# Output projection by token tiles with all its weights on chip, and the norms of the last three token halves behind the last value product

## The chip, the cores and the metric

The kernel runs on one core of a Trainium2 chip. The metric is device time in microseconds for one execution of the whole program; lower is better. The core has five engines that run side by side, each through its own list of instructions in order: TensorE (PE; its weight loads are shown apart as PEld), VectorE (DVE), ScalarE (ACT), GpSimd (POOL) and SyncE (SP), which here only issues DMAs. They are held together by semaphores that the kernel writes out by hand.

## What is computed

One decoder layer over 1024 tokens and 16 meta tokens of width 1024: a norm, one input projection, eight heads of stick-breaking attention (64 wide) and four heads of a gated linear recurrence (128 wide), a norm over each head, one output projection that is added to the input, a second norm, and a SwiGLU feed-forward of width 2816.

```python
o_sb = stick_breaking_attention(sb_q, sb_k, sb_v)            # 8 heads x 64
o_sb = group_rmsnorm(merge_heads(o_sb), sb_norm_g, SB_HEADS)
o_hg = hgrn2_chunkwise(hg_q, hg_k, hg_i, log_f)              # 4 heads x 128
o_hg = group_rmsnorm(merge_heads(o_hg), hg_norm_g, HG_HEADS) * jax.nn.silu(hg_g)
mix = jnp.concatenate([o_sb, o_hg], axis=-1) @ w_out
h = h + mix
u2 = rmsnorm(h, norm2_g)
ffn = (jax.nn.silu(u2 @ w_gate) * (u2 @ w_up)) @ w_down
return rmsnorm(h + ffn, final_norm_g)                        # the 1024 tokens
```

All matmuls are of float32 precision: each operand is split into a rounded high part and the rest as a low part (type fp32r), and a product is three matmuls, high with high, high with low, low with high.

## The kernel before

**The last pair of heads.** Attention runs over pairs of heads and, in a pair, over 14 pieces of a query block (`PIECES`, n = 0 to 55). TensorE makes scores (L973), transposes the weights of a piece (`turn`, L990) and multiplies them with the values (`values`, L1010); ScalarE makes two sigmoids of the scores (L1104, L1107) and copies the transposes out (L1131, L1133); VectorE scans a running product (L1158) and weighs (L1165). A half of the tokens of a pair, number e = 0 to 7, is complete every seven pieces. Its head norm then goes: ScalarE squares the output and copies it to `mixed` (`out_evac`, L1114, L1115), TensorE sums (L1040), ScalarE takes the root (`head_norm_scalar`, L1054), VectorE inverts and widens (`head_norm_widen`, L1061, L1063), TensorE transposes (L1047), VectorE scales `mixed` (`head_norm_finish`, L1071). `SUMS_AT` and `SPREAD_AT` (L130, L131) say at which piece; e = 5 and 6 fall into the last pair, e = 7 behind the loop. Finished halves of `mixed` are split into `tok_hi` (ScalarE, L1085) and `tok_lo` (VectorE, L1090), two at a piece (`SPLIT_AT`, L1078): 15 of 16 in the loop, the last behind it.

**The output projection.** Behind the loop TensorE runs 32 groups of 12 matmuls (`out_group` at L1928, `out_part`, L335 to L337) as four passes c = 0 to 3 over all eight token tiles t: the passes 0 and 1 make the left 512 columns (first the recurrence heads' half of the contraction, then the attention heads'), 2 and 3 the right 512. A pass uses one chunk of `w_out` of 1 MB, called ("O", c). It is loaded by SyncE into `w_raw` (L477), copied to `w_hi` by ScalarE (`high_chunk`, L482), and its rest goes to `w_lo` by VectorE (`low_chunk`, L500). There are two slots, so chunk 2 is split when pass 0 is over and chunk 3 when pass 1 is. The next load into `w_raw` waits for the split before. After pass 1 and pass 3 VectorE adds a token tile's bank to `h_res` (`add`, L1649), which GpSimd has filled with x after the last value product (L1309).

**The second norm.** For a token tile whose row is complete: ScalarE squares with a running sum and takes the root (`stats`, L1437, L1440), VectorE inverts and scales (`scale`, L1654, L1658), TensorE transposes (`second_transposes`, L1947), ScalarE copies out twice, rounded and whole (`high`, L1449, L1452), VectorE makes the low part (`low`, L1671). All rows are complete only in pass 3. SyncE spills `h_res` to memory (L1209), since its place is used again.

**The feed-forward's first half.** A scheme of seven products for four (`P1` to `P7`, `PRODUCTS` at L135) is applied to blocks of the gate and up weights, n = 0, 2, ... gate and n = 1, 3, ... up. A product is 12 matmuls (L1977, L1979, L1980). Each needs a block of weights, or a sum of blocks (`weight_sums`, `weight_sum4`: L1715, L1718, L1721, L1727), rounded by ScalarE (`block_high`, L1393) and completed by VectorE (`block_low`, L1705) into a ring of ten, and tokens or sums of tokens (t1 to t4). The token sums are made by VectorE over all tiles at once (`token_sum`, L1696), rounded by ScalarE (`high_t`, L1463); the low parts are made by VectorE for t2 (L1685) and by GpSimd for t3 and t4 (L1320). Raw blocks come through two buffers, and the load for n = 2 waits for `block_low(12)`, the last use of n = 0. P1(2) also waits for `weigh_f(0, 2)` (L1762), the product of the gated part with the bank that it writes anew. The order of all this is written out by hand, once for each engine; that of TensorE is

```python
for c in range(4):
    for t in range(TT):
        ...
        out_group(c, t)
        ...
        if c == 3 and t >= 4:
            second_transposes(t - 3)
...
second_transposes(5); p1(0); second_transposes(6); p2(0); second_transposes(7)
p1(1); p2(1); p5(0); p5(1); p3(0); p3(1); p6(0); p6(1); p7(0); p7(1); p4(0)
```

(the last two lines stand one call to a line in the code). After them the loop over n = 2 to 21 takes its steady form.

## Time and profile before

| | |
|---|---|
| median of 3 runs | 1391.59 us (1389.67 to 1391.77) |
| profiled execution | 1388.97 us, its span 1387.2 us |
| TensorE busy | 1317.5 us, 95% |
| VectorE, ScalarE, GpSimd busy | 59%, 40%, 3% |
| mean granted clock of TensorE | 0.99 |

The profile is of one execution. Times in its rows count from the start of the span; durations are of one instruction, or of a merged row from its first start to its last end. Two instructions of one engine overlap a little, so a row's duration is larger than the distance from start to start. "[7.15 <-DVE h_res L1762]" says that the engine sat idle for 7.15 us before, and what it seems to have waited for.

### The profile page before, as it was taken

What the parts mean: (1) busy time and instruction counts of PE and PEld (TensorE: products, weight loads), DVE (VectorE), ACT (ScalarE), POOL (GpSimd) and SP (SyncE); (2) the same over time, 40 slices, a digit from 0 to 9 for tenths busy, and PEclk for the clock granted to TensorE, in tenths of its full rate; (3) what the DMA queues carried; (4) which work ended last, traced back from release to release, by engine and by line L of the source; (5) the groups of instructions that cost most, each with busy time, mean ns of one, the idle gap of its engine ahead of it and who ended that gap; (6) DMA issues with size and microseconds to landing.
All of it is one profiled execution on the core that took longest, in us unless ns stands there. A gap on an engine that the chain in (4) does not pass through costs nothing.

```text
span 1387.2 us, 23036 instructions
## 1 busy us (share of the span) xinstructions
PE 1317.5 (95%) x9428; PEld 1086.9 (78%) x9428; DVE 819.3 (59%) x1334; ACT 554.8 (40%) x1027; POOL 38.7 (3%) x64
## 2 busy tenths in 40 slices
PE   5999999999899999879987999999999999999998
PEld 5898989898567767458866888888888888888886
DVE  6376766763787565852486665655666646335413
ACT  6323332331676455851374333333333334324311
POOL 4000000000000000010003000000000000000000
PEclk9999999999999999999998999999999999999999
DMA  6211111011001000031322222122222239626601
GB/s 199 61 32 31 32 31 32 32 32 31 2 32 32 2 32 2 32 138 62 110 86 76 92 84 82 63 92 91 91 91 71 74 121 343 212 75 217 231 23 61
DMA packets 77496, 112.18 MB, mean 81 GB/s; under 512 B 3776, under 2 KB 52928, under 8 KB 77392
## 3 DMA queue, kind: packets, MB, share of 16 engines
q1 hardware_dynamic: 74528, 100.74, 21.8%
q0 software_dynamic: 2864, 9.97, 2.0%
q8 instruction: 75, 1.23, 0.4%
q14 instruction: 29, 0.24, 0.1%
HBM read 90.78 MB, written 19.92 MB: 80 GB/s over the span
## 4 chain that ended last, share of the span: by engine, by line
PE 88%; ACT 6%; DVE 4%; issue 2%; DMA 1%; ACTq 0%; DVEq 0%; POOLq 0%
PE ps L1977 10%; PE ps L1980 9%; PE ps L1979 9%; PE ps L323 8%; PE ps L325 8%; PE ps L324 8%; PE ps L2065 6%; PE ps L2066 6%; PE ps L2064 6%; PE ps L1010 3%; PE ps L973 2%; PE ps L614 2%; PE ps L990 2%; PE ps L335 2%; PE ps L337 2%
## 5 line engine op out<-in xcount | busy, mean ns | idle before, releaser
L323 PE MATMUL ps<-a_hi,w_hi 128*128 128x352 f32 (+2 forms) x576 | 207.8, 361 | 7.5 <-DVE a_lo L441 2.9
L325 PE MATMUL ps<-a_hi,w_lo 128*128 128x352 f32 (+2 forms) x576 | 200.0, 347 | 0.0
L324 PE MATMUL ps<-a_lo,w_hi 128*128 128x352 f32 (+2 forms) x576 | 199.9, 347 | 0.0
L323 PEld LDWEIGHTS ps<-a_hi,w_hi 128*128 128x128 f32 x576 | 109.2, 190 | 20.2 <-DVE a_lo L441 3.3
L1977 PE MATMUL ps<-a_hi,w_hi 128*128 128x512 f32 x288 | 114.4, 397 | 9.9 <-DVE h_res L1762 7.2
L325 PEld LDWEIGHTS ps<-a_hi,w_lo 128*128 128x128 f32 x576 | 109.1, 189 | 8.3
L324 PEld LDWEIGHTS ps<-a_lo,w_hi 128*128 128x128 f32 x576 | 109.3, 190 | 7.3
L1979 PE MATMUL ps<-a_lo,w_hi 128*128 128x512 f32 x288 | 113.5, 394 | 0.0
L1980 PE MATMUL ps<-a_hi,w_lo 128*128 128x512 f32 x288 | 113.4, 394 | 0.0
L2064 PE MATMUL ps<-a_hi,w_hi 128*128 128x512 f32 x288 | 112.0, 389 | 0.0
L2065 PE MATMUL ps<-a_lo,w_hi 128*128 128x512 f32 x288 | 112.0, 389 | 0.0
L2066 PE MATMUL ps<-a_hi,w_lo 128*128 128x512 f32 x288 | 112.0, 389 | 0.0
L1158 DVE TENSOR_TENSOR_SCAN beta<-beta,ones 128x272 f32<-128x272 f32 (+5 forms) x112 | 92.9, 870 | 15.7 <-ACT beta L1104 15.7
L500 DVE TENSOR_TENSOR w_lo<-w_raw,w_hi 128x2048 fp32r<-128x2048 f32 (+1 forms) x22 | 41.8, 1902 | 75.3 <-ACT w_hi L482 75.3
L1977 PE MATMUL ps<-t_hi,w_hi 128*128 128x512 f32 x208 | 81.0, 390 | 0.6 <-POOL t_lo L1320 0.6
L1980 PE MATMUL ps<-t_hi,w_lo 128*128 128x512 f32 x208 | 80.9, 389 | 0.0
L1979 PE MATMUL ps<-t_lo,w_hi 128*128 128x512 f32 x208 | 80.9, 389 | 0.0
L1977 PEld LDWEIGHTS ps<-a_hi,w_hi 128*128 128x128 f32 x288 | 55.0, 191 | 22.5 <-DVE h_res L1762 7.6
L1980 PEld LDWEIGHTS ps<-a_hi,w_lo 128*128 128x128 f32 x288 | 54.9, 191 | 11.7
L1979 PEld LDWEIGHTS ps<-a_lo,w_hi 128*128 128x128 f32 x288 | 55.1, 191 | 11.4
L2064 PEld LDWEIGHTS ps<-a_hi,w_hi 128*128 128x128 f32 x288 | 54.1, 188 | 11.3
L2065 PEld LDWEIGHTS ps<-a_lo,w_hi 128*128 128x128 f32 x288 | 54.1, 188 | 11.2
(274 smaller groups left out, 2557.3 us busy)
## 6 DMA issues: line engine op xcount, KB each, us to landing
w_raw<-in_w_in_dram SPq DMA_DIRECT2D x24, 512.0 KB
w_raw<-in_w_gate_dram SPq DMA_DIRECT2D x11, 1024.0 KB, 5.5
h_res<-in_w_up_dram SPq DMA_DIRECT2D x11, 1024.0 KB, 5.4
f_spill<-h_res SPq DMA_DIRECT2D x44, 256.0 KB, 2.0
h_res<-in_w_down_dram SPq DMA_DIRECT2D x22, 512.0 KB, 5.7
w_raw<-f_spill SPq DMA_DIRECT2D x30, 256.0 KB, 4.2
w_raw<-in_w_down_dram SPq DMA_DIRECT2D x11, 512.0 KB, 4.9
h_norm<-in_w_down_dram SPq DMA_DIRECT2D x11, 512.0 KB, 5.7
```

Of the source, the lines that this page charges most:

```text
L323: nc.tensor.matmul(psum, wh, ah, start=k == 0, stop=False)
L324: nc.tensor.matmul(psum, wh, al, start=False, stop=False)
L325: last = nc.tensor.matmul(psum, wl, ah, start=False, stop=k == KT - 1)
L500: last = nc.vector.tensor_tensor(w_lo[:, s, c], w_raw[:, c], w_hi[:, s, c].bitcast(F32), ALU.subtract)
L1010: last = nc.tensor.matmul(dst, v, probs_t[:, par, i * P:(i + 1) * P], start=hi == width and i == 0, stop=lo == 0 and i == len(tiles) - 1)
L1158: nc.vector.tensor_tensor_scan(c, c, ones[:, 0:1].to_broadcast([P, hi - lo]), begin, ALU.mult, ALU.mult).then_inc(scanned.sem, 1)
L1977: nc.tensor.matmul(psum, wh[:, c], yh[:, k], start=start and k == 0, stop=False, skip_group_check=not start)
L1979: nc.tensor.matmul(psum, wh[:, c], yl[:, k], start=False, stop=False, skip_group_check=not start)
L1980: last = nc.tensor.matmul(psum, wl[:, c], yh[:, k], start=False, stop=k == UNIT - 1, skip_group_check=not start)
L2064: nc.tensor.matmul(psum, fh[:, a], tok_hi[:, q % 8, half], start=start, stop=False)
L2065: nc.tensor.matmul(psum, fh[:, a], tok_lo[:, q % 8, half], start=False, stop=False)
L2066: return nc.tensor.matmul(psum, fl[:, a], tok_hi[:, q % 8, half], start=False, stop=stop)
```

## The change

Three things are changed together.

*The last norms.* For e = 5, 6 and 7 ScalarE no longer takes the root in its place; for 5 and 6 it copies the eight sums to `kept`. Behind the last value product it takes the roots of all three, VectorE inverts and widens all three, TensorE transposes twelve times after the third projection group, and VectorE finishes the three halves, which are then split (three splits behind the loop instead of one).

*The output projection.* Chunks 2 and 3 of `w_out` get slots of their own (in the places of t3 and t2), and the groups run in the order `OUT_SEQ`: the left columns of tiles 0 to 3 as two passes, tile 4's left, then the right columns tile by tile for 0 to 4, then tiles 5, 6 and 7 each with all four groups. Banks follow `ADD_BANK`. The sums, the norm and the transposes of a tile run as soon as its row is complete; `n2_rows` has two rows instead of four.

*The first products.* The ring of ten is turned by eight places, `sum1` has a second place for n = 1, the token sums are made tile by tile, and the low parts of t3 and t4 are made by VectorE. The written orders of ScalarE and VectorE between the projection and the steady loop are new.

```diff
-SPREAD_AT = {n + 2: e for n, e in SUMS_AT.items()}
+SPREAD_AT = {n + 2: e for n, e in SUMS_AT.items() if e < 5}
+LAST_HALVES = [6, 5, 7]
...
+OUT_SEQ = [(t, c) for c in (0, 1) for t in range(4)] + [(4, 0), (4, 1)] + \
+    [(t, c) for t in range(4) for c in (2, 3)] + [(4, 2), (4, 3)] + [(t, c) for t in (5, 6, 7) for c in range(4)]
...
+ADD_BANK = dict(zip(ADDS, [0, 1, 2, 3, 4, 5, 6, 7, 5, 6, 7, 4, 5, 6, 7, 4]))
...
+        def last_norms_scalar(act):
+            act.wait_ge(s_sum.sem, s_sum.done(8))
+            nc.scalar.activation(kept_of(7), bank(7, 8), ACT.Sqrt, scale=1.0 / SB_DIM, bias=eps).then_inc(s_root.sem, 1)
+            nc.scalar.activation(kept[:, 0:16], kept[:, 0:16], ACT.Sqrt, scale=1.0 / SB_DIM, bias=eps)\
+                .then_inc(s_root.sem, 1)
+
+        def last_norms_widen(dve):
+            dve.wait_ge(s_root.sem, s_root.done(9))
+            nc.vector.reciprocal(kept, kept).then_inc(s_inv.sem, 1)
+            dve.wait_ge(s_inv.sem, s_inv.done(6))
+            for e in LAST_HALVES:
+                nc.vector.tensor_copy(WIDE[e].rearrange("p (c t) -> p c t", c=2 * UNIT),
...
         def head_norm_scalar(act, e, psum):
             act.wait_ge(s_sum.sem, s_sum.done(e + 1))
+            if e >= 5:
+                nc.scalar.activation(kept_of(e), psum, ACT.Copy).then_inc(s_root.sem, 1)
+                return
...
-                low_t(Y12, t3_hi, t3_lo, UNIT, t3_done)
-                low_t(Y22, t4_hi, t4_lo, 2 * UNIT, t4_done)
...
-                high_chunk(act, ("O", 1))
-                high_chunk(act, ("O", 2), (o_proj, TT))
-                high_chunk(act, ("O", 3), (o_proj, 2 * TT))
+                high_chunk(act, ("O", 2), (t_done, 2 * NP))
+                act.wait_ge(m_lo.sem, 16)
+                high_chunk(act, ("O", 3), (t_done, 2 * NP))
...
+                for t in range(3):
+                    high_t(Y12, t3_hi, t3_sum, t3_high, t)
+                hold_p1(1)
+                block_high(12)
+                high_t(Y11, t2_hi, t2_sum, t2_high, 3)
+                high_t(Y12, t3_hi, t3_sum, t3_high, 3)
                 act.wait_ge(t2_done.sem, t2_done.done(UNIT))
-                high_t(Y22, t4_hi)
-                hold_u2(1)
+                act.wait_ge(t4_sum.sem, t4_sum.done(UNIT))
+                for t in range(4):
+                    high_t(Y22, t4_hi, t4_sum, t4_high, t)
+                hold_p5(0)
+                hold_p5(1)
                 block_high(13)
...
+                block_low(6)
+                add(7, 1)
                 scale(7)
...
+                low(7)
+                low_t1(3)
+                token_sums(3)
                 block_low(10)
                 block_low(11)
+                for t in range(3):
+                    low_t(Y12, t3_hi, t3_lo, t3_high, t3_done, t)
                 block_low(12)
+                low_t(Y11, t2_hi, t2_lo, t2_high, t2_done, 3)
+                low_t(Y12, t3_hi, t3_lo, t3_high, t3_done, 3)
+                c11(1)
+                for t in range(4):
+                    low_t(Y22, t4_hi, t4_lo, t4_high, t4_done, t)
                 c22(0)
                 c12(0)
                 block_low(13)
...
+                for n, (t, c) in enumerate(OUT_SEQ):
+                    if n == 1:
+                        head_norm_tensor(pe, 7, "sums", bank(7, 8))
+                    if n == 3:
+                        last_norms_tensor(pe)
+                    if n == 2 * UNIT:
+                        pe.wait_ge(s_mixed.sem, 8)
+                    out_group(t, c)
+                    if c == 3 and 1 <= t <= 4:
+                        second_transposes(t - 1)
+                    if c == 1 and t >= 5:
+                        second_transposes(t - 1)
...
-                second_transposes(5)
                 p1(0)
-                second_transposes(6)
                 p2(0)
                 second_transposes(7)
```

## Rows read from the trace of the kernel before

**Rows 1.** The page: busy us, share of the span, instructions.

```profile
PE 1317.5 (95%) x9428; PEld 1086.9 (78%) x9428; DVE 819.3 (59%) x1334; ACT 554.8 (40%) x1027; POOL 38.7 (3%) x64
```

**Rows 2.** Windows: busy us (instructions) by engine, clock, DMA share and GB/s.

```profile
560.00:607.00 47.00, 32.54 (x571) 20.64 (x569) 38.68 (x63) 40.58 (x88) 0.00 (x0) 0.93 0.07 24
607.00:705.00 98.00, 94.20 (x468) 77.70 (x468) 37.12 (x50) 28.60 (x49) 4.98 (x9) 1.00 0.36 129
705.00:770.00 65.00, 54.93 (x228) 43.99 (x229) 51.67 (x69) 35.39 (x65) 14.28 (x9) 0.89 0.19 66
770.00:1100.00 330.00, 330.00 (x1457) 273.27 (x1456) 201.07 (x313) 115.86 (x208) 0.00 (x0) 1.00 0.26 84
```

**Rows 3.** TensorE's waits, 540 to 830: us in total, times, longest.

```profile
PE ps L1977 <- DVE h_res L1762: 7.2, 1, 7.2
PE ps L1947 <- ACT y_first L1452: 2.4, 1, 2.4
...
PE ps L1977 <- DVE a_lo L1678: 1.4, 1, 1.4
...
PE ps L1977 <- POOL t_lo L1320: 0.6, 1, 0.6
```

**Rows 4.** Timeline of ScalarE in the last pair: start, us, line, operation, tiles.

```profile
564.10 1.28 ACT L1054 ACT_TABLE_LOAD   x1
565.39 0.27 ACT L1054 ACTIVATE small<-ps,small 128x8 f32<-128x8 f32 x1
...
566.17 1.28 ACT L1104 ACT_TABLE_LOAD   x1
...
594.79 1.19 ACT L1085 ACTIVATE a_hi<-mixed 128x512 fp32r<-128x512 f32 x2
```

**Rows 5.** Timeline of VectorE there: a stretch without a wait between first and last.

```profile
567.99 1.81 DVE L1158 TENSOR_TENSOR_SCAN beta<-beta,ones 128x384 f32<-128x384 f32 x2 [1.63 <-ACT beta L1104]
...
571.83 0.74 DVE L1071 SCALAR_TENSOR_TENSOR mixed<-mixed,small,ps 128x512 f32<-128x512 f32 x1
...
592.57 0.43 DVE L1063 COPY gain<-small 128x512 f32<-128x512 f32 x1
...
602.22 0.68 DVE L1090 TENSOR_TENSOR a_lo<-mixed,a_hi 128x512 fp32r<-128x512 f32 x1
```

**Rows 6.** Timeline of TensorE at the projection's start, and its four transposes.

```profile
607.89 0.47 PE L335 MATMUL ps<-w_hi,a_hi 128*128 128x512 f32 x1 [1.33 <-issue]
...
616.77 0.60 PE L1047 MATMUL ps<-ident,gain 128*128 128x128 f32 x4
617.13 0.48 PE L335 MATMUL ps<-w_hi,a_hi 128*128 128x512 f32 x1
```

**Rows 7.** DMA issues: destination, source, count, KB each, median us to landing.

```profile
w_raw<-in_w_gate_dram SPq DMA_DIRECT2D x11, 1024.0 KB, 5.5
...
h_res<-in_x_dram POOLq DMA_DIRECT2D x8, 512.0 KB, 8.0
```

**Rows 8.** Timeline of VectorE between projection and steady loop.

```profile
620.66 2.29 DVE L500 TENSOR_TENSOR w_lo<-w_raw,w_hi 128x2048 fp32r<-128x2048 f32 x1 [1.11 <-ACT w_hi L482]
...
681.48 1.29 DVE L1658 SCALAR_TENSOR_TENSOR n_rows<-h_res,small,gain 128x1024 f32<-128x1024 f32 x1
...
734.54 1.78 DVE L1705 TENSOR_TENSOR w_lo<-w_raw,w_hi 128x512 fp32r<-128x512 f32 x1
...
750.90 2.68 DVE L1762 TENSOR_TENSOR h_res<-h_res,h_norm 128x512 f32<-128x512 f32 x4
```

**Rows 9.** Timeline of ScalarE in the same stretch.

```profile
678.02 1.06 ACT L1437 ACTIVATE n_junk<-h_res 128x1024 f32<-128x1024 f32 x1 [2.24 <-DVE h_res L1649]
...
745.10 0.63 ACT L1393 ACTIVATE w_hi<-w_raw 128x512 fp32r<-128x512 f32 x1 [5.81 <-DMA w_raw<-in_w_gate_dram]
```

**Rows 10.** Windows, columns as in rows 2: after a short and after a long wait.

```profile
592.00:594.00 2.00, 0.63 (x4) 0.42 (x4) 1.97 (x5) 1.99 (x6) 0.00 (x0) 1.00 0.00 0
...
752.00:760.00 8.00, 5.17 (x12) 4.08 (x13) 6.47 (x11) 0.74 (x2) 0.00 (x0) 0.51 0.38 139
```

More of the change, by code:

```diff
@@ L182, in hybrid_layer @@
         table_load = small[:, 72:73]
+        kept = small[:, 72:96]
         meta_decay = sb("meta_decay", [P, 2 * META])
@@ L310, in hybrid_layer @@
         UNITS = [(h, half) for h in range(HG_HEADS) for half in range(2)]
-        slots = [(w_hi[:, 0], w_lo[:, 0]), (w_hi[:, 1], w_lo[:, 1])]
-        OUT_BANKS = [0, 1, 2, 3, 4, 6, 5, 7]
+        slots = [(w_hi[:, 0], w_lo[:, 0]), (w_hi[:, 1], w_lo[:, 1])] + \
+            [[t[:].rearrange("p k n -> p (k n)") for t in pair] for pair in ((t3_hi, t3_lo), (t2_hi, t2_lo))]
         def turned_group(weights, tile, cols, psum, a_hi=act_hi, a_lo=act_lo, steps=range(KT)):
@@ L1177, in attention_vector @@
                     nc.vector.tensor_copy(turned_to(1, w), turned(1, w)).then_inc(pt_second.sem, 1)
-                if n - 1 in SUMS_AT:
+                if SUMS_AT.get(n - 1, 5) < 5:
                     head_norm_widen(dve, SUMS_AT[n - 1])
@@ L1231, in _ @@
                 load_raw(0)
-                for t in range(4):
+                for t in range(2):
                     spill_h(t)
@@ L1237, in _ @@
                 load_raw(1)
-                for t in range(4, TT):
+                for t in range(2, TT):
                     spill_h(t)
@@ L1469, in _ @@
+                stats(0)
+                stats(1)
+                high(0)
+                stats(2)
+                high(1)
+                stats(3)
+                high(2)
+                stats(4)
+                high(3)
+                act.wait_ge(n2_normed.sem, n2_normed.done(4))
+                act.wait_ge(x_came[2].sem, 32)
+                act.wait_ge(x_came[3].sem, 32)
                 block_high(0)
                 block_high(1)
-                stats(0)
-                stats(1)
@@ L1762, in weigh_f @@
                     nc.vector.tensor_tensor(u, u, src, ALU.mult).then_inc(weighed[i].sem, 1)
-                low_chunk(dve, ("O", 1))
+                add(0, 0)
                 low_chunk(dve, ("O", 2))
-                for t in range(TT):
-                    add(0, t)
+                add(1, 0)
+                add(2, 0)
+                add(3, 0)
                 low_chunk(dve, ("O", 3))
+                add(4, 0)
                 dve.wait_ge(gain2.sem, 16)
+                add(0, 1)
+                scale(0)
@@ L1770, in _ @@
+                add(1, 1)
+                scale(1)
+                low(0)
+                add(2, 1)
+                scale(2)
+                low(1)
+                add(3, 1)
+                scale(3)
+                low(2)
+                add(4, 1)
+                scale(4)
+                low(3)
                 block_low(0)
                 block_low(1)
-                add(1, 0)
                 weight_sums(0)
                 weight_sum4(0)
-                add(1, 1)
-                scale(0)
@@ L1777, in _ @@
-                add(1, 2)
-                scale(1)
-                low(0)
-                add(1, 3)
-                scale(2)
-                add(1, 4)
-                scale(3)
-                low(1)
-                add(1, 5)
-                scale(4)
-                low(2)
-                add(1, 6)
-                scale(5)
-                low(3)
+                add(5, 0)
+                low(4)
+                first_sums(1)
+                low_t1(0)
+                token_sums(0)
@@ L1791, in _ @@
+                add(5, 1)
+                scale(5)
+                add(6, 0)
+                low(5)
+                low_t1(1)
+                token_sums(1)
+                add(6, 1)
+                scale(6)
                 block_low(2)
-                add(1, 7)
-                scale(6)
-                low(4)
                 block_low(3)
-                scale(7)
-                low(5)
-                block_low(4)
-                weight_sums(1)
-                low(6)
-                low_t1(0)
@@ L1802, in _ @@
-                weight_sum4(1)
-                block_low(5)
-                low(7)
-                low_t1(1)
-                low_t1(2)
-                low_t1(3)
-                token_sum(0)
-                block_low(6)
+                block_low(4)
+                add(7, 0)
+                second_sum(1)
+                weight_sum4(1)
+                low(6)
+                block_low(5)
+                low_t1(2)
+                token_sums(2)
+                block_low(6)
+                add(7, 1)
```

253 lines of the change are left out of this document (124 added, 129 removed).

## Prediction

> **What bounds the kernel now.** I read the page's busy shares first, then the granted clock and busy time by stage, then TensorE's waits, then the timelines of the places where it waits. TensorE is busy 95% of the span [rows 1], so a change can only pay where it is idle or slow. By stage [rows 2] that is two places: the last pair of heads (560 to 607 us: TensorE 32.5 us of 47, ScalarE 40.6, VectorE 38.7) and the first products of the feed-forward (705 to 770: 54.9 of 65, clock 0.89). The output projection between them is full (94.2 of 98), and from 770 on TensorE is busy without a gap (330.0 of 330). So the projection itself, 384 matmuls, has nothing to give: the change keeps its matmuls and their shapes. What it can give lies on either side of it.
>
> On the right side TensorE waits 7.2 us for one VectorE product, 2.4 us for ScalarE, 1.4 us for VectorE's `a_lo` and 0.6 us for GpSimd's `t_lo` [rows 3], with 0.9 us of issue between; after the long wait twelve matmuls start every 0.43 us instead of 0.23.
>
> **Part 1: the norms of the last three token halves.** In the last pair two head norms (e = 5 and 6) fall into the loop. Each makes ScalarE load the Sqrt table, take a 128x8 root and load the Sigmoid table back: 1.28 + 0.27 + 1.28 us [rows 4]. The change puts a 128x8 Copy in the root's place; no trace shows it, the nearest row is the 128x8 root itself, 0.27 us, so the root and the copy cancel and four loads go, 5.1 us. (Bounds: a Copy that cost nothing adds 0.5, one that cost as much as a 128x512 split, 0.6 us, takes 0.7.) One of ScalarE's splits (0.52 us from start to start, half of the x2 row in [rows 4]) also leaves the loop. A second one left stood behind the last sigmoids and was hidden. ScalarE loses 5.6 us.
>
> Does the stage's end move by that? The chain of waits goes through ScalarE from 564 to 599.6 almost without a break, but VectorE is busy without a break from 567.99 to 602.9 as well [rows 5]. Its first scan waited for ScalarE's sigmoid behind the two table loads, and so starts 2.5 us earlier. Within the stretch it loses two finishes (0.74 us each, 0.66 from start to start), one widening (reciprocal and copy, 0.56) and one split (0.60): 2.5 us. VectorE therefore gives 5.0 us and ScalarE 5.6, and the turning of the last pieces lags behind the scans by 2 to 5 us, which absorbs the difference. I take 5.4 us, bounds 3.5 (VectorE sets it and a piece's turn is lost) and 6.2. Two finishes, two widenings and eight transposes come back after the last value product. They are covered: TensorE has three projection groups of 2.73 us to run from 607.89 before it needs them [rows 6], in which today ScalarE and VectorE only wait; three widenings of 0.43 and a larger reciprocal end some 6 us after that start, and the transposes come at 8.6 to 8.9. The transposes themselves are on TensorE: four cost 0.44 us here (616.77 to 617.13, and a slower first matmul), so eight more cost 0.8. What stands behind them is tight: the fourteenth split ends 12.7 us after the start and group (0,1), now fifth, wants it at 12.5 to 13.0, a wait of 0 to 0.3 us that I leave at nothing; each further us of delay in the chain transposes, finish, split would be paid in full.
>
> The Trainium skill ("ScalarE: Activation LUTs", What ACT_TABLE_LOAD costs) agrees with the 1.28 us of a load but adds a drain of about 1.38 us to each switch; here the root starts 1.29 us after the load and the load follows the copy before it at once, so no drain shows. By the page's 2.66 us four switches would be worth 10.6 us (estimate) instead of 5.1. I go by the rows.
>
> **Part 2: weights on chip.** Chunks 2 and 3 get buffers of their own, so their splits no longer wait for the projection's passes. They must now arrive early, since token tile 0 wants all four. Counting from the first projection matmul: chunk 1 is split on ScalarE by 5.7 and on VectorE by 8.1 (1.9 us, and 2.3 in [rows 8]); the load of chunk 2 is issued then, but eight loads of x of 512 KB, 8.0 us each to land, fill the DMA engines until about 12 us [rows 7], so I give it 7.5 us instead of the 5.5 of a load of 1 MB. Chunk 2 is on chip at 19.9, chunk 3 (5.5 + 1.9 + 2.3) at 29.7. TensorE needs chunk 2 at 29.1 and chunk 3 at 31.9. Cost nothing, with 2.2 us of cover; a load later by more than that is paid in full.
>
> **Part 3: sums, norms and the first products.** The adds, statistics (1.06 us Square and a root, 1.48 to the end [rows 9]) and scalings (1.29 [rows 8], 1.45 with the reciprocal) of tokens 0 to 4 now run under groups of later tiles, where before all eight stood in the last pass. GpSimd's eight `t_lo` go to VectorE, at 0.60 us from start to start: 4.8 us more for VectorE. But while GpSimd ran them, three `block_low` took 1.78 us each instead of 0.68 [rows 8]; that goes, 3.3 us.
>
> I walked the written order of the engines from the first projection matmul, each step at the durations above. The same walk for the old order gives P1(2) its start at 754.2 against 754.8 in the trace. In the new order TensorE has these stalls left:
> - before transposes 5, 0.6 us (add, statistics and scaling of tile 5 against two groups);
> - before P1(0), 1.6: the last group's sum has a `block_low` before it on VectorE, and P1 waits for all sixteen sums;
> - before P3(0), 1.9: ScalarE's copy of P5(0) is queued behind four t4 roundings, which wait for VectorE's last t2 part;
> - before P1(2), 3.2. After P7(0) VectorE has thirteen operations in line (two sums with banks, three `block_low`, three weight sums, four products, then the product P1(2) waits for), 8.4 us at 0.60 to 0.72 and 0.3 for the hand-overs, against 5.5 us of P7(1) and P4(0).
>
> This last stall is 7.2 us today because the gate block for it is asked for after `block_low(12)` ends at 739.7, lands 5.4 us later [rows 9], and only then come the rounding, the Sigmoid table and the four products (2.68 us for four products in [rows 8]). In the new order `block_low(12)` ends 113 us after the first projection matmul, where it now ends at 132, so the block has landed before P3 is over and the table is loaded under P3(1).
>
> The clock: after the 7.2 us wait it stood at half (1.2 GHz) for nearly all of 752 to 760 [rows 10], P1(2) took 5.2 us instead of 2.73. After the 2.1 us wait at 591 to 593 it stayed at 2.4 GHz [rows 10]. A wait of 3.2 us lies between: 0 to 2.5 us, I take 1.2.
>
> **The sum.** Today's losses: waits 2.4 + 0.9 + 1.4 + 0.6 + 7.2 = 12.5, low clock 1.5 (seven matmuls of P1(0)) + 2.5, together 16.5. New: 0.6 + 1.6 + 1.9 + 3.2 + 1.2 = 8.5, and 0.8 of transposes. Right side: 16.5 - 9.3 = 7.2 us. With part 1: 7.2 + 5.4 = 12.6. The walk without rounding the small gaps gives 8.2 for the right side; I take 13 in all. Behind P1(2) nothing changes: the steady loop is TensorE's. The profiled execution took 1389.0 us (span 1387.2 and 1.8 around it) and would take 1376.0; the median of the runs is 1391.6, 2.6 above it, and would become 1378.6.
>
> **The rivals.**
> - *The stage of the last heads does not give what the table loads cost.* VectorE's unbroken stretch speaks for it, ScalarE's part in the chain against. If only the 2.5 us ahead of the first scan come through: 13 - 2.9 = 10.1, 1381.5.
> - *The stall before P1(2) stays*, since its last link is VectorE's order behind P7(0), with the clock at half again and 5 us or more idle: 2 to 4 us less, 1381 to 1383. For it: VectorE's queue ahead of it is longer than before by the t4 parts. Against: those end 13 us before P7(0) does.
> - *The stalls close almost wholly* and the clock stays up: 4 us more, 1374.5. The walk's steps are accurate to some 0.6 us each, and three stalls are below 2.
> - *Slower: the weights come late.* From 29.1 us on, tile 0 stands first and the whole order is behind it. If chunk 2's load were held back by the loads of x and chunk 3's by the same amount, beyond 2.2 us of cover for both together, the wait is paid once, before group (0,3). To end over 0.2% slower the two loads would have to be later by 13 + 2.2 + 2.8 = 18 us, 9 us each and so 14.5 to 16.5 us long instead of the 5.5 to 8.0 that [rows 7] show. With 6 us more it is 1382, with 18 us 1394.5.
> - *It does nothing*: TensorE's work is the same, and if the reordering only moved the waits, 1391.
>
> **How the numbers follow.** Forecast 0.66; closing stalls 0.10; the heads giving half 0.09; the stall staying 0.09; late weights, mild 0.02; nothing 0.02; late weights, slower 0.02. The range takes in the closing stalls, both unknown costs and the two cases around 1382: 1373 to 1384. A time within 0.2% (2.8 us, about what a measurement of this kernel can tell from no change) needs two of the bad cases at once or a load late by some 12 us: 0.03. Slower 0.03, faster 0.94.
>
> **What would show it.** Right: in 560 to 607 only one Sqrt load remains (the last), VectorE's stretch starts near 565.5, and the first projection matmul comes at 602.5. No TensorE wait for `w_lo` in the projection, transposes between the groups. No GpSimd `t_lo`, every `block_low` at 0.68. The gate block for n = 2 is issued about 18 us earlier against the projection's start, and the wait before P1(2) is about 3 us. Wrong: a wait of TensorE before group (0,3) for chunk 3, a granted clock below 1 inside the projection, or a stage of heads that ends later than 604.

## The result, and the profile of the changed kernel

The changed kernel takes 1380.1 us (median of four, 1379.3 to 1381.5) against 1390.9 (1389.7 to 1391.8) beside it: ratio 0.9924, 95% interval 0.9907 to 0.9941, 10.8 us faster. The forecast was 1378.6, 13 us faster. Measured again on another chip it was 1379.6 against 1390.0, ratio 0.9919 (0.9896 to 0.9941). The profiled execution took 1381.45 us, the longest of its four, with a span of 1379.7 us and a mean granted clock of 0.985; that of the kernel before took 1388.97 us, near the short end of its times (1388.4 to 1393.8 over all rounds). So the two profiles lie only 7.5 us apart.

Busy us, share and instructions of each engine, to set beside [rows 1]:

```profile
PE 1319.8 (96%) x9428; PEld 1089.1 (79%) x9428; DVE 821.6 (60%) x1349; ACT 549.9 (40%) x1024; POOL 24.8 (2%) x56
```

TensorE's work is the same, GpSimd has lost 14 us of it, ScalarE 5, VectorE has 2 more. TensorE's waits in the changed kernel, from 520 to 800 us (us in total, times, longest), against [rows 3]:

```profile
PE ps L2044 <- issue: 3.7, 2, 2.0
PE ps L2044 <- DVE h_res L1811: 3.0, 1, 3.0
...
PE ps L2015 <- DVE n_rows L1703: 0.5, 1, 0.5
```

The wait of 7.2 us before P1(2) is 3.0 us. The one for `y_first`, the one for `a_lo` and the one for GpSimd's `t_lo` are gone. The two waits of `issue`, before P1(0) and P3(0), have grown from 0.9 and 0.4 to 1.7 and 2.0 us, and there is one of 0.5 us before the transposes of tile 5. The timeline has these, and the projection's start (start us, us, line, operation, tiles, idle before):

```profile
604.53 0.77 PE L343 MATMUL ps<-w_hi,a_hi 128*128 128x512 f32 x1 [1.33 <-issue]
```

```profile
704.15 0.47 PE L2044 MATMUL ps<-a_hi,ring_more 128*128 128x512 f32 x1 [1.68 <-issue]
...
723.60 0.47 PE L2044 MATMUL ps<-a_hi,w_hi 128*128 128x512 f32 x1 [1.98 <-issue]
```

The first of these rows, the projection's first matmul, already holds the surprise. It took 0.47 us in [rows 6] and takes 0.77 here. The granted clock of three stretches says why; it is the column before the DMA share:

```profile
600.00:608.00 8.00, 5.90 (x39) 4.58 (x36) 0.56 (x1) 2.86 (x4) 3.39 (x7) 0.58 0.24 82
724.00:728.00 4.00, 4.00 (x12) 3.11 (x11) 0.41 (x1) 2.11 (x3) 0.00 (x0) 0.57 0.24 79
748.00:752.00 4.00, 4.00 (x13) 3.09 (x12) 3.15 (x6) 0.00 (x0) 0.00 (x0) 0.57 0.12 45
```

Behind the waits around the last values (1.9, 0.8 and 1.3 us), behind P3(0)'s 1.98 us and behind P1(2)'s 3.0 us TensorE ran at half its clock (1.2 GHz) for most of 7, 4 and 4 us. In the one profile of the kernel before, the clock was at 1.00 at the start of the projection.

To say where the time went I cut each profile at three places: the last copy of `bq` at 560.53 in the kernel before (the start of the last pair), the first projection matmul, and ScalarE's copy of the bank behind P1(2), which is the row at 760.21 before and at 752.16 after. In the changed kernel these two ScalarE rows are:

```profile
562.48 0.60 ACT L582 ACTIVATE bq<-ps 128x512 f32<-128x512 f32 x1 [2.08 <-PE ps L333]
...
752.16 0.60 ACT L1442 ACTIVATE h_norm<-ps 128x512 f32<-128x512 f32 x1 [5.45 <-PE ps L2047]
```

| kernel | up to last pair | last pair | projection to P1(2) | rest |
|---|---|---|---|---|
| before | 560.5 | 47.4 | 152.3 | 627.0 |
| changed | 562.5 | 42.1 | 147.6 | 627.5 |
| changed, again | 561.0 | 43.1 | 147.5 | 627.6 |
| norms alone | 560.3 | 42.1 | 154.2 | 627.0 |
| tiles alone | 561.1 | 49.0 | 145.3 | 627.0 |
| low parts on GpSimd | 560.0 | 42.3 | 150.7 | 627.0 |
| chunk 3 late | 560.8 | 43.1 | 153.3 | 627.6 |
| new order | 559.9 | 42.3 | 143.9 | 627.5 |
| fillers everywhere | 560.9 | 41.5 | 143.4 | 627.6 |
| fillers around heads | 560.4 | 41.5 | 144.8 | 627.6 |
| fillers before gate | 560.0 | 42.2 | 145.6 | 627.6 |
| order and fillers | 560.3 | 41.5 | 141.8 | 627.6 |
| order and fillers, again | 559.9 | 41.5 | 141.2 | 627.6 |

The first column moves by 2.6 us although nothing in front of it is edited in any of these kernels: it is longer where a low stretch of the clock falls into the loop over heads (near 352 and 492 us in the first profile of the changed kernel). So the stages are to be compared, not the spans: 5.3 us came from the last pair and 4.7 from projection to P1(2), against 5.4 and 7.2 to 8.2 forecast.

### The profile page after: what moved, and what is told of

It is laid out like the page before. It is cut to its first block, busy times and chain, and to the rows that moved or that the text cites. A ratio compares the mean times of both kernels' runs of the same rounds, so it can differ in the third digit from the quotient of the medians.

```text
span 1379.7 us, 23039 instructions
## 1 busy us (share of the span) xinstructions
PE 1319.8 (96%) x9428; PEld 1089.1 (79%) x9428; DVE 821.6 (60%) x1349; ACT 549.9 (40%) x1024; POOL 24.8 (2%) x56
## 4 chain that ended last, share of the span: by engine, by line
PE 91%; ACT 3%; DVE 3%; issue 2%; DMA 1%; ACTq 0%; DVEq 0%; POOLq 0%
PE ps L2044 10%; PE ps L2047 10%; PE ps L2046 10%; PE ps L331 9%; PE ps L333 8%; PE ps L332 8%; PE ps L2130 6%; PE ps L2131 6%; PE ps L2129 6%; PE ps L1020 3%; PE ps L983 2%; PE ps L343 2%; PE ps L624 2%; PE ps L344 2%; PE ps L345 2%
## 5 line engine op out<-in xcount | busy, mean ns | idle before, releaser
L2044 PE MATMUL ps<-a_hi,w_hi 128*128 128x512 f32 x280 | 110.6, 395 | 5.0 <-DVE h_res L1811 3.0
L332 PEld LDWEIGHTS ps<-a_lo,w_hi 128*128 128x128 f32 x576 | 109.6, 190 | 7.2
L2129 PE MATMUL ps<-a_hi,w_hi 128*128 128x512 f32 x288 | 112.0, 389 | 0.0
L2130 PE MATMUL ps<-a_lo,w_hi 128*128 128x512 f32 x288 | 112.0, 389 | 0.0
L2131 PE MATMUL ps<-a_hi,w_lo 128*128 128x512 f32 x288 | 112.0, 389 | 0.0
L2047 PE MATMUL ps<-a_hi,w_lo 128*128 128x512 f32 x280 | 110.3, 394 | 0.0
L2046 PE MATMUL ps<-a_lo,w_hi 128*128 128x512 f32 x280 | 110.0, 393 | 0.0
L510 DVE TENSOR_TENSOR w_lo<-w_raw,w_hi 128x2048 fp32r<-128x2048 f32 (+1 forms) x20 | 37.3, 1864 | 63.4 <-ACT w_hi L492 63.3
L1227 DVE COPY probs_t<-ps 128x384 f32<-128x384 f32 (+2 forms) x44 | 25.3, 575 | 63.5 <-PE ps L1000 63.2
L2129 PEld LDWEIGHTS ps<-a_hi,w_hi 128*128 128x128 f32 x288 | 54.0, 188 | 11.3
L2130 PEld LDWEIGHTS ps<-a_lo,w_hi 128*128 128x128 f32 x288 | 54.1, 188 | 11.2
```

The lines of the kernel that those rows point to most:

```text
L332: nc.tensor.matmul(psum, wh, al, start=False, stop=False)
L510: last = nc.vector.tensor_tensor(lo_[:, c], w_raw[:, c], hi_[:, c].bitcast(F32), ALU.subtract)
L2044: nc.tensor.matmul(psum, wh[:, c], yh[:, k], start=start and k == 0, stop=False, skip_group_check=not start)
L2046: nc.tensor.matmul(psum, wh[:, c], yl[:, k], start=False, stop=False, skip_group_check=not start)
L2047: last = nc.tensor.matmul(psum, wl[:, c], yh[:, k], start=False, stop=k == UNIT - 1, skip_group_check=not start)
L2129: nc.tensor.matmul(psum, fh[:, a], tok_hi[:, q % 8, half], start=start, stop=False)
```

## The experiments

**The two parts apart.** The first kernel has the norms finished late and everything else as before:

```diff
-SPREAD_AT = {n + 2: e for n, e in SUMS_AT.items()}
+SPREAD_AT = {n + 2: e for n, e in SUMS_AT.items() if e < 5}
...
```

> The kernel before with the part on the norms alone: the last three token halves of heads are finished together behind the last value product, in their own banks; the projection by groups of two halves, chunks 2 and 3 of w_out split as before, and GpSimd's token parts stay. My theory: the stage of the last pair gets 5.3 us shorter, as it did in the whole change, eight more transposes behind it cost 0.8 us, so 1390.9 becomes about 1386.4 (1385.5 to 1388; at the upper end if the low clock at the start of the projection comes with this part, 1.7 us). One Sqrt load between the last pair's softmax and the first projection matmul instead of five. Rival 1 (the stage gains only because the projection's evacuations by tiles make room there): 0 to -1.5 us. Rival 2 (this part is the whole gain, the tiles give nothing): -10 us or more, 1381.

Measured: 1386.9 us against 1391.1, ratio 0.9967 (0.9955 to 0.998), 4.6 us by the ratio (2.8 to 6.3). The last pair is 5.3 us shorter, as in the whole change. From the projection to P1(2) it is 1.9 us longer, and that arises ahead of P1(0), which starts 2.3 us later against the projection's start: the transposes (0.8 forecast) and a low clock at the start. Its first projection matmul:

```profile
602.32 0.77 PE L337 MATMUL ps<-w_hi,a_hi 128*128 128x512 f32 x1 [1.33 <-issue]
```

That is 0.77 again. VectorE's wait before P1(2) is untouched (7.2 us).

The second kernel has the norms of before in the changed kernel:

```diff
-SPREAD_AT = {n + 2: e for n, e in SUMS_AT.items() if e < 5}
+SPREAD_AT = {n + 2: e for n, e in SUMS_AT.items()}
...
-                        last_norms_tensor(pe)
+                        head_norm_tensor(pe, 7, "spread", bank(7))
...
```

> The changed kernel with the norms of before: every token half's norm is finished inside the loop over heads, the last one alone behind it; the projection by token tiles, its early chunks and VectorE's token parts stay as changed. My theory: the two parts are independent, so the gains of this run and of the norms alone add up to the whole (10.8 us within 1 us); from first projection matmul to the last product group the walk is 4.7 us shorter, as in the whole change, or 6 if the low clock at the start of the projection belongs to the norms. 1385 to 1386.5. Rival 1 (the parts need one another: the late norms delay the first group by tiles, so that its gain is eaten): -2 us or less, 1389. Rival 2 (the tiles are the whole gain): -9 us or more, 1382.

Measured: 1383.9 us, ratio 0.9952 (0.9936 to 0.9969), 6.7 us. Its own stage is 7.0 us shorter than before (152.3 to 145.3) and 2.3 us shorter than in the whole change: its profile has no low clock behind P3(0), which is worth 1.6 us (the table further down), and P1(0) starts 0.7 us sooner, with eight transposes fewer ahead of it. Its last pair is 1.7 us longer than before, with more low clock inside (0.84 from 560 to 600 us, before 0.91). Its first projection matmul, and the window around it:

```profile
610.09 0.77 PE L343 MATMUL ps<-w_hi,a_hi 128*128 128x512 f32 x1 [1.33 <-issue]
```

```profile
607.00:614.00 7.00, 5.43 (x21) 4.30 (x22) 0.10 (x1) 2.40 (x4) 3.82 (x8) 0.52 0.30 116
```

So the low clock at the start of the projection also comes with the norms of before. That the change brought it is not shown: it stands in all nine profiles of kernels that have the change or a part of it and no added matmuls ahead of the projection, and the only profile of the kernel before, which lacks it, is of one execution. The two parts add up: 4.6 + 6.7 = 11.3, the whole change 10.8 and 11.3. Within the width of these intervals neither part needs the other, and neither is the whole gain. The part that I had costed at 5.4 - 0.8 is worth 4.6.

**GpSimd's low parts.** The eight operations go back to GpSimd:

```diff
...
-                for t in range(4):
-                    low_t(Y22, t4_hi, t4_lo, t4_high, t4_done, t)
+                for t in range(4):
+                    pool_low(Y22, t4_hi, t4_lo, t4_high, t4_done, t)
...
```

> The changed kernel with the low parts of the token tiles (eight operations, t3 and t4) on GpSimd again as before, everything else as changed. Theory A (VectorE's subtractions and GpSimd's disturb one another: block_low took 1.78 us beside GpSimd's work and 0.68 without): the block_low operations beside them take 1.78 us again, and c22(0) and the low parts of t4 come 2 to 3 us later than now; the waits before P3(0) and P1(2) grow, 1 to 4 us slower than the changed kernel, 1381 to 1384. Rival B (that contention was covered: in that stretch VectorE stands idle for 14.7 us and gets rid of eight operations of 0.60 us): within 0.5 us, or up to 2 us faster, because the queue before P1(2) loses four operations.

Measured: 1382.6 us against 1379.6 for the changed kernel on the same chip, 3.0 us slower (ratios to before 0.9944, 0.9926 to 0.9961, and 0.9919, 0.9896 to 0.9941; the intervals overlap a little, the single times, 1381.7 and more against 1381.1 and less, do not). GpSimd, VectorE and TensorE of this kernel (the three timelines):

```profile
713.99 6.72 POOL L1369 TENSOR_TENSOR t_lo<-h_res,t_hi 128x512 fp32r<-128x512 f32 x4 [7.39 <-ACT t_hi L1513]
```

```profile
716.09 1.78 DVE L1759 TENSOR_TENSOR ring_more<-w_raw,ring_more 128x512 fp32r<-128x512 f32 x1
...
717.79 1.77 DVE L1759 TENSOR_TENSOR ring_more<-h_res,ring_more 128x512 fp32r<-128x512 f32 x1
...
719.49 1.77 DVE L1759 TENSOR_TENSOR w_lo<-w_raw,w_hi 128x512 fp32r<-128x512 f32 x1
```

```profile
724.66 0.76 PE L2049 MATMUL ps<-a_hi,w_hi 128*128 128x512 f32 x1 [4.35 <-issue]
```

While GpSimd runs, each `block_low` takes 1.78 us, as in [rows 8]; without it 0.69. The wait before P3(0) is 4.35 instead of 1.97 us, 2.4 more, and nothing later gives that back. The path is VectorE's last t2 part (721.17, against P1(0) 2.4 us later than in the changed kernel), ScalarE's four t4 roundings, which wait for it, and the copy of P5(0) behind them. Theory A holds, with its place: the contention is on the path through P3(0), not before P1(2), whose wait stays 3.0 us. The Trainium skill ("SBUF — State Buffer", SBUF: two separate sides) says that a VectorE operation with two SBUF inputs and a GpSimd operation that reads SBUF exclude one another for a whole instruction. The trace agrees: VectorE's operations take 1.1 us more than their 0.7, and GpSimd's four take 6.7 us, where its next four, with VectorE idle, take 5.0.

**Weights that are late.** ScalarE's rounding of chunk 3 waits until eleven projection groups are done, the last of them (0,2), just ahead of the first that wants the chunk (the expectation calls it the third group, which it is of tile 0 alone):

```diff
-                high_chunk(act, ("O", 3), (t_done, 2 * NP))
+                high_chunk(act, ("O", 3), (o_proj, 11))
```

> The changed kernel with one wait changed: ScalarE's rounding of chunk 3 of w_out waits for the third group of the projection instead of the last softmax sums, so its low part comes about 4.3 us later than the first product that wants it (the cover in the changed kernel is 2 to 3 us). Nothing is added or left out. Theory A (weights that are late are paid for in full, since TensorE bounds this stage): a wait for w_lo of 4 to 5 us before that group, with a low clock behind it 1.7 more, 4 to 6.5 us slower than the changed kernel, 1384 to 1386.5. Rival B (the lag is taken up by the waits before P1(0), P3(0) and P1(2), 6.7 us in all, which are there in any case): less than 2 us slower.

Measured: 1385.7 us, 6.1 us slower than the changed kernel on the same chip (ratio to before 0.9968). TensorE's timeline, and the window behind the wait:

```profile
642.05 0.79 PE L343 MATMUL ps<-t_hi,a_hi 128*128 128x512 f32 x1 [4.68 <-DVE t_lo L510]
```

```profile
636.00:648.00 12.00, 7.32 (x22) 5.46 (x21) 3.24 (x3) 1.91 (x1) 0.00 (x0) 0.72 0.29 89
```

The stage from projection to P1(2) is 5.9 us longer than in the changed kernel (153.3 and 147.5). By the start times it is 4.7 of wait and 2.8 for the low stretch behind it, less 1.6 because this profile has no low clock behind P3(0). The three later waits stay at 1.7, 2.0 and 3.0 us, so they took up nothing. A late weight is paid in full, as the prediction's slower rival had it; only the weights were not late in the changed kernel.

**The low clock.** Added matmuls keep TensorE running where it waits. They write a bank that is free there and compute nothing of the result:

```diff
+        def keep_busy(count, psum, source):
+            for _ in range(count):
+                nc.tensor.matmul(psum, source[:, 0:P], source[:, 0:HALF], start=True, stop=True)
```

> The changed kernel with added matmuls of 128x512 that write a bank nobody reads afterwards, placed where TensorE waits: 8, 3 and 5 around the last pair of heads, 6 before P1(0), 8 before P3(0), 12 before P1(2). They compute nothing of the result. Theory A (the low clock after each wait is what my sum left out, 5 us in three stretches: 601 to 608, 724 to 728, 748 to 752): the granted clock stays at 1.00 behind the three waits and the kernel gets 3.4 to 5 us faster than the changed one, 1375 to 1377. Rival B (the low stretches cost nothing, because VectorE or ScalarE bounds the work just behind each wait too): within 0.7 us of the changed kernel, 1380. Rival C (the fillers stand in the way of the products that they precede: 0.216 us each at most at the full clock beyond the wait): 1 to 2 us slower, 1382.

Measured: 1375.0 us, ratio 0.9889 (0.9872 to 0.9906), against 0.9924 and 0.9919 for the changed kernel: 4.2 to 4.9 us faster than it. The clock at the three places (windows of this kernel; 716 to 724 and 736 to 748 hold P3(0) and P1(2)):

```profile
596.00:608.00 12.00, 12.00 (x106) 8.85 (x107) 3.70 (x9) 5.58 (x8) 4.22 (x8) 1.00 0.33 124
716.00:724.00 8.00, 7.85 (x35) 6.23 (x34) 5.17 (x9) 4.66 (x8) 0.00 (x0) 1.00 0.42 131
736.00:748.00 12.00, 11.72 (x52) 9.38 (x51) 10.14 (x17) 5.17 (x10) 0.00 (x0) 1.00 0.41 133
```

The clock stays at full speed, and the stage takes 143.4 us instead of 147.6. The waits themselves are not shorter, only filled. So the low clock cost 4.2 us of this stage, and 0.6 more in the last pair (42.1 to 41.5). Theory A, and rivals B and C fall.

What each stretch costs can be read from the starts of the same matmuls in several profiles (us; "low" where a low stretch falls in):

| kernel | projection to P1(0) | to P3(0) | to P1(2) | to ScalarE's copy |
|---|---|---|---|---|
| changed | 99.62 low | 19.45 | 23.91 low | 4.65 low |
| changed, again | 99.48 low | 19.44 | 23.91 low | 4.63 low |
| tiles alone | 98.95 low | 19.44 | 22.29 | 4.59 low |
| fillers around heads | 98.40 | 19.43 | 22.31 | 4.64 low |
| new order | 100.58 low | 19.43 | 20.77 | 3.07 |

The rows for P3(0) and P1(2) in the changed kernel are at 723.60 above and at 747.51, in the kernel with fillers around the heads here:

```profile
747.51 0.50 PE L2044 MATMUL ps<-a_hi,w_hi 128*128 128x512 f32 x1 [3.00 <-DVE h_res L1811]
```

```profile
719.69 0.47 PE L2055 MATMUL ps<-a_hi,w_hi 128*128 128x512 f32 x1 [1.97 <-issue]
...
742.00 0.79 PE L2055 MATMUL ps<-a_hi,w_hi 128*128 128x512 f32 x1 [2.99 <-DVE h_res L1822]
```

With the same waits the stretch behind P3(0) costs 1.6 us (23.9 and 22.3), that behind P1(2) 1.6 (4.7 and 3.1), and that at the start 1.2 in the changed kernel and 2.2 in the new order's profile, where it reaches further into the projection (the new order's 20.77 has 1.5 us less wait in it). Together that is 4.4 in the changed kernel, against the 4.2 that the fillers took away.

> The changed kernel with the added matmuls around the last pair of heads alone (8, 3 and 5 of 128x512, into a bank nobody reads; they compute nothing of the result). Theory A (the low clock from 601 to 608 us is the price of the waits of 1.94, 0.77 and 1.33 us just before the projection, half of its length): clock 1.00 at the start of the projection and 1.7 us faster than the changed kernel, ratio 0.991, about 1378.5; the low stretches behind P3(0) and P1(2) stay. Rival B (the low stretch only moves, to the next wait): no gain, 1380.

Measured: 1375.9 us, ratio 0.9893 (0.988 to 0.9906), by the ratios 3.6 to 4.3 us less than the changed kernel, where I had said 1.7. Three things are in it. The last pair is 41.5 instead of 42.1 and 43.1 us. The projection starts at full clock (first row):

```profile
600.00:608.00 8.00, 8.00 (x72) 6.03 (x69) 1.81 (x5) 4.64 (x6) 4.24 (x8) 1.00 0.52 210
716.00:724.00 8.00, 6.03 (x27) 4.70 (x26) 4.49 (x8) 5.36 (x9) 0.00 (x0) 1.00 0.43 131
738.00:748.00 10.00, 7.01 (x24) 5.36 (x23) 7.54 (x13) 3.51 (x7) 0.00 (x0) 0.83 0.43 151
```

And the clock behind P3(0) stayed up too (second row), with the same wait of 1.97 us and no filler there. Only the stretch behind P1(2) is left (third row). The stage took 144.8 us, 2.8 less than in the changed kernel: 1.2 at the start and 1.6 behind P3(0). That second part was not the fillers' doing as far as is shown.

> The changed kernel with the added matmuls before P1(0), P3(0) and P1(2) alone (6, 8 and 12). Theory A (each low stretch has its own price and its own cause): the stretches behind P3(0) and P1(2) go, 3.4 us faster than the changed kernel, ratio 0.990, about 1376.7, and with the kernel that fills only around the heads the gains add up to the 5.1 us of both together. Rival B (no more than one of the two is won, because the fillers before P1(2) delay it): 1.7 us, 1378.4.

Measured: 1377.3 us, ratio 0.9902 (0.9889 to 0.9915). The stage took 145.6 us, 2.2 more than with no low stretch: that is the price of the one at the start, the only one it has, and 1.0 more than in the first profile of the changed kernel, where the stretch is shorter (6.8 against 10.2 us). The other two are gone, for 3.2 us, where 3.4 was forecast. By the ratios it is 2.4 to 3.1 us faster than the changed kernel. The gains of these two kernels add up to more than that of the first one (6.0 to 7.4 against 4.2 to 4.9), since each also lost the stretch behind P3(0).

**VectorE's order.** Nothing added, the order changed before P1(2):

```diff
-                c22(0)
-                c12(0)
...
+                c22(0)
+                c12(0)
```

(The two combined parts go behind `block_low(13)`, the sums of weights and the first two weighings. The edit also puts `weigh_f(0, 2)`, the product that P1(2) waits for, ahead of `block_low(15)`, which the expectation does not name.)

> The changed kernel with only the order of VectorE's work before P1(2) changed: block_low(13), the sums of weights for group 2 and the weighing of tiles (0,0) and (1,0) go ahead of the combined token parts c22(0) and c12(0). Nothing is added or left out. Theory A (the wait of 3.0 us before P1(2) is VectorE's queue: it stands idle for 14.7 us and then has 13 operations in a row in front of the last weighing): the wait falls to about 1.5 us, and the kernel is 1.5 us faster than the changed one (3.1 if the clock stays up with it), 1377 to 1378.6. Rival B (what VectorE waits for in those 14.7 us is the gate's own chain, the load of w_gate for n=2 and its rounding by ScalarE, so the order behind it decides nothing): within 0.5 us, 1380. Rival C (c22(0) comes too late for P3 of the next group): 1 us or more slower.

Measured: 1375.6 us, ratio 0.9893 (0.9877 to 0.991), by the ratios 3.6 to 4.3 us less than the changed kernel, where theory A said 1.5 to 3.1. VectorE in the changed kernel, and then in this one, where it fills its idle time (timelines):

```profile
739.11 0.69 DVE L1795 TENSOR_TENSOR h_norm<-h_norm,ps 128x512 f32<-128x512 f32 x1 [14.71 <-PE ps L2047]
...
746.78 0.68 DVE L1811 TENSOR_TENSOR h_res<-h_res,ps 128x512 f32<-128x512 f32 x1
```

```profile
727.61 1.48 DVE L1811 TENSOR_TENSOR h_res<-h_res,h_norm 128x512 f32<-128x512 f32 x2
...
736.05 0.69 DVE L1795 TENSOR_TENSOR h_norm<-h_norm,ps 128x512 f32<-128x512 f32 x1 [6.95 <-PE ps L2047]
...
742.18 0.69 DVE L1811 TENSOR_TENSOR h_res<-h_res,ps 128x512 f32<-128x512 f32 x1 [3.05 <-ACT h_res L1470]
```

And TensorE's waits of this kernel:

```profile
PE ps L2044 <- issue: 3.7, 2, 2.0
...
PE ps L2044 <- DVE h_res L1811: 1.5, 1, 1.5
```

The idle stretch of 14.7 us is 7.0, the row that P1(2) waits for now itself waits for ScalarE, and TensorE's wait is 1.5 us as forecast. Which of the moved operations did it the runs do not tell apart. Behind a wait of 1.5 us the clock stayed up. In the first profile it stayed up behind P3(0) as well, although that wait was 1.96 us.

> The kernel with VectorE's new order once more, for one open point: in its first profile the clock stayed up behind P3(0) too, although the wait there was 1.96 us as in the changed kernel. Theory A (the order of VectorE's work cannot reach that wait, so it was how the execution fell): the low stretch behind P3(0) is there in this profile, or single times spread by 1.7 us around 1376.5. Rival B (it goes with this order in every execution): no low stretch from 715 to 760 us again, and times within 1.3 us, 1375.5.

Measured: one of the six executions, the profiled one, took 1391.7 us, and its clock column stands at 0.95 outside the low stretches from the first loads to the end; the ratio of 0.9921 (0.9892 to 0.995) has it in it. It lies 14.4 us behind the first profile at the start of the last pair, 11.7 of them by 266 us, and none is added behind P1(2) (627.5 us, as elsewhere). The other five took 1376.2 to 1378.5, median 1377.6, 0.9906 of the kernel before, 2 us more than the first time. The stretch behind P3(0), at 736.98 in this profile, is low again:

```profile
736.00:744.00 8.00, 7.02 (x24) 5.61 (x25) 5.75 (x9) 3.92 (x6) 0.00 (x0) 0.76 0.30 103
```

So VectorE's order does not decide it, and the new order is worth 2 to 4 us by how that falls (1.6 us); 3.1 us (1.5 of wait, 1.6 of clock) is what its mechanism explains. Theory A.

**Both edits together.**

> The changed kernel with both of the earlier edits: VectorE's new order before P1(2), and added matmuls that compute nothing of the result where TensorE waits (16 around the last pair of heads, 6, 8 and 6 before P1(0), P3(0) and P1(2)). The earlier two gave 1375.0 and 1375.6 us each. Theory A (each of the two keeps the clock up behind the last waits, so that part of their gains is the same gain): the fillers add to the new order only the low stretch at the start of the projection, 1.7 us, and the new order adds to the fillers only the wait, 1.5 us: 1373.4 to 1374. Rival B (independent gains of 5.1 and 4.6 us add up): 1370.5. Rival C (with the wait at 1.5 us the 6 and 8 fillers stand in the way): 1375 or more.

> The kernel with both edits (new order, added matmuls that compute nothing of the result) once more, beside the one with the order alone: 1373.6 us as before, ratio 0.988, 1.7 to 2 us faster than the order alone, which is the low stretch at the start of the projection. If it is under 1 us, the fillers are worth nothing beside the new order.

Measured: 1373.6 us, ratio 0.9878 (0.9861 to 0.9895), and again 1372.2, ratio 0.9868 (0.9854 to 0.9882). The stage takes 141.8 us, 1.6 less than with the fillers alone and 2.1 less than with the order alone: theory A, the gains share the low stretches behind P1(2) and P3(0). In the second round it was 5.4 us faster than the order alone, where I had said 1.7 to 2; the last pair (41.5 against 42.3) and the stage (141.2 against 143.9) explain 3.5 of that, and the stretch behind P3(0), 1.6 us, which the order alone has in some executions, goes the same way. This is the fastest kernel here, 16 to 18 us under the kernel before and 6 to 8 under the changed one.

## Why the prediction came out as it did

- *What bounds it.* Right. The projection gave nothing of its own, the rest behind P1(2) is 627.0 and 627.5 us, and all of the gain lies in the two stages named.
- *Part 1, forecast 5.4 us.* The last pair is 5.3 us shorter. VectorE's unbroken stretch started at 567.04, which is 565.1 on the old scale (forecast 565.5), the first projection matmul came at 604.53, on that scale 602.6 (forecast 602.5), and one Sqrt load is left, at 604.33. The two kept copies took 0.18 and 0.53 us, and the operation behind each started 0.05 us after it, near the bound at which a copy costs nothing. That the stage agrees to 0.1 us is partly luck: the clock is in it on both sides. The second profile of the same kernel gave 4.3 us, the kernels without a low stretch at its end 5.9, and the profile of before has a low stretch in it that no run prices.
- *Eight transposes, 0.8 us, and the tight split*: no wait for `a_lo` showed in the projection.
- *Part 2, cost nothing.* Right in this kernel, but with less behind it than I had said. Chunk 2 was ready 21.3 us after the first projection matmul (forecast 19.9), chunk 3 30.8 (29.7), since chunk 1, behind which their loads are issued, was split 9.7 us after that start instead of 8.1; the loads themselves took 7.3 and 5.3 us (7.5 and 5.5). TensorE got to group (0,3) at 33.7 us instead of 31.9, because the low clock had held it up. Where the fillers took the low clock away, chunk 1 was split after 8.0 us as forecast, but the load of chunk 2 then took 10.5 us instead of 7.5, from 610.39 to ScalarE's start at 620.85, beside the loads of x (7.9 us each to land, 6.5 in the changed kernel); chunk 3 was ready at 32.4 and the cover was gone:

```profile
634.81 0.50 PE L343 MATMUL ps<-t_hi,a_hi 128*128 128x512 f32 x1 [0.34 <-DVE t_lo L510]
```

```profile
620.85 1.92 ACT L492 ACTIVATE t_hi<-w_raw 128x2048 fp32r<-128x2048 f32 x1 [6.21 <-DMA w_raw<-in_w_out_dram]
```

  The 2.2 us of cover were really 0.3 us short, as the rival of the late weights had it, in the mild form. One error, the low clock that was left out, hid the other.
- *Part 3, the waits.* Forecast 0.6, 1.6, 1.9 and 3.2 us, measured 0.5, 1.7, 2.0 and 3.0. The walk through the written orders named each wait's place and size. On the side of before the sum left out a second wait of `issue`, 0.4 us before P3(0) (12.9 instead of 12.5 us of waits). The gate load for n = 2 was issued 115.7 us after the first projection matmul instead of 131.8, 16 us earlier (forecast 18).
- *The clock: the term that failed.* The prediction put "0 to 2.5 us, I take 1.2" behind one wait, P1(2)'s. Measured, low stretches cost 4.2 us of the stage by the fillers, 4.4 by the start times: 1.2 at the start of the projection, 1.6 behind P3(0) and 1.6 behind P1(2). The size behind P1(2) was about right. The other two were not in the sum at all, since I read from [rows 10] that a wait of 2.1 us costs nothing, one row of one execution. The same profile had a second case between 2.1 and 7.2 us, in the last pair, which the prediction did not take in; there the clock fell:

```profile
569.80 1.12 PE L1010 MATMUL ps<-probs_t,bv 128*64 128x128 f32 x8 [2.64 <-ACT probs_t L1133]
```

```profile
568.00:576.00 8.00, 6.20 (x70) 3.84 (x78) 8.00 (x14) 7.41 (x20) 0.00 (x0) 0.57 0.01 2
```

  Of the prediction's signs of being wrong this one came: a granted clock below 1 inside the projection. Without the low clock the stage takes 143.4 us, 8.9 less than before, against 8.2 of the walk with its 1.2 of clock in it, so 9.4.
- *The rivals.* "The stalls close almost wholly" and "the stall before P1(2) stays" both did not come; the stall came as walked. Nor did the heads give only half. The late weights were shown to work as written (4.7 us late gave 6.1), and did not occur in the changed kernel.

The two stages together give 5.3 and 4.7, the latter 8.9 less 4.2 of clock: 10.0 us, within the interval of the measured 10.8 (8.2 to 12.9). The forecast of 13 lay 3 us above that, as much as the clock that it left out (4.2 less 1.2). That the profiled execution shows only 7.5 us in its time is the low clock in its loop over heads, 2 us ahead of any edit, and 0.5 us in the rest that I have no cause for.

What moves the end of the last pair by 1 us (42.1 and 43.1 us for the same kernel) the profiles do show: where the low stretch ahead of the projection begins. It begins about 36 us behind the copy of `bq` in the two profiles with 43.1 us in the table (changed again, chunk 3 late), 38 to 39 us behind it in those with 42.1 to 42.3, and where the fillers keep it away the last pair takes 41.5.

What stays open: why the low clock behind the wait of 2.0 us comes in some executions and not in others, and whether the kernel before has the stretch at the projection's start in executions other than its profiled one.

## What to carry to other kernels

Walk the written order of every engine when work is moved between them; here it gave four waits to 0.2 us. Then look at every place where the bounding engine waits in the new order, one by one, for the clock behind it: here the waits around the projection's start and the one before P3(0), none above 2 us, were taken for free and cost 2.8 us of clock. One profile does not say that a wait is free. A cover worked out from an engine's pace holds only for that pace; the fix that speeds the engine up spends it.

## What the runs showed of the hardware

- A low clock behind short waits is partly chance. Behind P1(0)'s wait of 1.7 us it came in none of eight profiles of kernels with the changed order (the changed kernel twice, tiles alone, low parts on GpSimd, chunk 3 late, new order twice, fillers around the heads). Behind P3(0)'s wait of 2.0 us it came in three of seven (the kernel with the low parts on GpSimd waits 4.35 us there, and has it), behind P1(2)'s 3.0 us in six of six, behind 1.5 us in neither of two. At the start of the projection, behind a row of waits of 0.8 to 2.0 us with short matmuls between, it came in nine of nine without fillers, but not in the profile of before. Each costs 1.1 to 2.2 us of the stage from projection to P1(2); the one at the start costs 0.6 to 1.6 more in the last pair.
- Matmuls that compute nothing can be worth their place: the changed kernel with them was 4.2 to 4.9 us faster.
- The clock column does not always tell the pace. In the profile of 1391.7 us it stands at 0.95 outside the low stretches, but only in the first part do matmuls of 128x512 start further apart (every 0.25 us at 60 us, against 0.23 in the first profile of that kernel); at 800 us they start every 0.227 us in both.
- Four `tensor_tensor` operations on GpSimd beside VectorE's cost VectorE up to 1.1 us for each of its operations that meets them, and themselves took 6.7 us instead of 5.0.
